# Adaptive-norm rows summed on VectorE instead of TensorE, and a projection moved into the recurrence, in a hybrid decoder layer

## What is computed

```python
mod = (c @ w_ada[l] + b_ada[l]).reshape(B, N_MOD, D)          # w_ada: 1024 x 6144
sh1, sc1, gt1, sh2, sc2, gt2 = [mod[:, i, None, :] for i in range(N_MOD)]
h = rms_norm(x, g_norm1[l]) * (1.0 + sc1) + sh1
proj = h @ w_in[l]
# branch A: short convolution, gated delta rule in chunks of 64 tokens -> o_a
# branch B: softmax attention with forget gates (fox)                   -> o_b
y = sigmoid(gate_a) * (o_a @ w_o_delta) + sigmoid(gate_b) * (o_b @ w_o_fox)
x = x + gt1 * (y @ w_out)
h = rms_norm(x, g_norm2[l]) * (1.0 + sc2) + sh2
x = x + gt2 * moe(h)          # 32 experts, top 4; then the final rms_norm
```

## Time and profile before

| | us |
|---|---|
| median of 3 runs | 1239.37 |
| lowest and highest | 1239.18, 1241.2 |
| the profiled execution, its own time | 1238.21 |
| span of its trace | 1236.4 |
| PE busy | 1138.6 (92%) |
| DVE busy | 316.1 (26%) |
| ACT busy | 184.7 (15%) |
| POOL busy | 106.0 (9%) |
| DMA, 462 MB in the main queue | 90.9% of 16 engines |

### The profile page before, as it was taken

One profiled execution on the slowest core, in us unless ns is written; L12 is line 12 of the kernel. 1 busy time (PEld: TensorE's weight loads), 2 busy tenths in 40 slices (PEclk: granted clock), 3 DMA queues, 4 the chain that ended last, 5 costly groups with the idle time before them and its releaser, 6 DMA issues.

```text
span 1236.4 us, 15283 instructions
## 1 busy us (share of the span) xinstructions
PE 1138.6 (92%) x6307; PEld 585.6 (47%) x6307; DVE 316.1 (26%) x674; ACT 184.7 (15%) x316; POOL 106.0 (9%) x50
## 2 busy tenths in 40 slices
PE   5999999999999999998989889898999999999896
PEld 2999799688543334333333323333434333333322
DVE  1633562131421221221212212121221222122102
ACT  2476344101310000010100000000000000000001
POOL 0764443110000000000000000000000000000000
PEclk9999999999999999999989999999999999999999
DMA  9963763597999999999999999999989999999995
GB/s 352 335 222 107 249 219 103 170 422 310 376 420 426 429 428 429 428 429 428 429 429 428 428 428 428 429 428 429 429 368 430 428 429 428 429 428 428 429 426 245
DMA packets 62558, 464.70 MB, mean 376 GB/s; under 512 B 8469, under 2 KB 31130, under 8 KB 34618
## 3 DMA queue, kind: packets, MB, share of 16 engines
q1 hardware_dynamic: 61256, 462.13, 90.9%
q10 hardware_dynamic: 1218, 1.93, 0.5%
q0 software_dynamic: 48, 0.13, 0.0%
HBM read 463.13 MB, written 1.05 MB: 375 GB/s over the span
## 4 chain that ended last, share of the span: by engine, by line
PE 64%; DMA 29%; issue 3%; ACT 2%; DVE 2%; SPq 0%; ACTq 0%; DVEq 0%
PE ps L488 61%; DMA ring<-in_w_down_dram 22%; DMA ring<-in_w_gate_up_dram 6%; PE ps L940 1%; ACT kept L1291 1%; DMA ring<-in_w_in_dram 1%; DMA ring<-in_g_onorm_dram 1%; PE ps L972 0%; PE ps L496 0%; ACT w_hi L1097 0%; DVE ring L1491 0%; SPq L358 0%; DVE ring L1485 0%; DVE ring L1775 0%; DVE kept L1717 0%
## 5 line engine op out<-in xcount | busy, mean ns | idle before, releaser
L488 PE MATMUL ps<-ring,kept 128*64 128x512 f32 (+1 forms) x3040 | 657.8, 600 | 36.1 <-DMA ring<-in_w_down_dram 22.5
L488 PEld LDWEIGHTS ps<-ring,kept 128*64 128x64 f32 (+1 forms) x3040 | 212.2, 138 | 454.3 <-issue 400.8
L488 PE MATMUL ps<-kept 128*128 128x128 f32 (+4 forms) x984 | 193.9, 413 | 8.5 <-ACT kept L1291 3.3
L488 PEld LDWEIGHTS ps<-kept 128*128 128x128 f32 (+2 forms) x984 | 108.5, 177 | 96.1 <-issue 81.0
L1287 ACT ACTIVATE kept<-kept 128x512 f32<-128x512 f32 x32 | 20.1, 629 | 731.4 <-DVE kept L1694 731.4
L1717 DVE TENSOR_TENSOR kept<-ps,kept 64x512 f32<-64x512 f32 x64 | 44.0, 688 | 298.4 <-PE ps L488 297.4
L1694 DVE TENSOR_SCALAR kept<-ps 128x512 f32<-128x512 f32 x32 | 22.1, 691 | 382.4 <-PE ps L488 382.4
L1787 POOL TENSOR_TENSOR w_lo<-ring,w_hi 128x1024 fp32r<-128x1024 f32 x38 | 91.8, 2434 | 108.2 <-ACT w_hi L1097 108.2
L488 PE MATMUL ps<-hT_hi,w_hi 128*128 128x256 f32 x272 | 78.7, 289 | 0.0
L488 PE MATMUL ps<-ring 64*64 64x64 f32 (+6 forms) x784 | 74.8, 270 | 3.0 <-issue 3.0
L488 PE MATMUL ps<-hT_lo,w_hi 128*128 128x256 f32 x272 | 77.0, 283 | 0.0
(11 more groups left out here) (227 smaller groups left out, 513.8 us busy)
## 6 DMA issues: line engine op xcount, KB each, us to landing
ring<-in_w_gate_up_dram SPq DMA_DIRECT2D x127, 2048.0 KB, 26.4
ring<-in_w_down_dram SPq DMA_DIRECT2D x47, 2048.0 KB, 23.8
kept<-in_w_down_dram SPq DMA_DIRECT2D x16, 2048.0 KB, 24.0
ring<-in_w_ada_dram SPq DMA_DIRECT2D x24, 1024.0 KB, 5.0
ring<-in_w_in_dram SPq DMA_DIRECT2D x22, 1024.0 KB, 11.5
ring<-in_w_out_dram SPq DMA_DIRECT2D x4, 1024.0 KB, 16.3
ring<-in_w_o_fox_dram SPq DMA_DIRECT2D x2, 1024.0 KB, 9.8
ring<-in_w_o_delta_dram SPq DMA_DIRECT2D x2, 1024.0 KB, 12.8
```

The source lines that it names most:

```text
L488: return pe.matmul(dst, lhsT, rhs, start=start, stop=stop, skip_group_check=True)
```

## The change

For ada part 1 and 2 DVE multiplies each unit (one row of `w_ada` in each partition) by its number of `c` and adds it to a running sum of 128x2048, `ada_sums` (`add_rows`: one TENSOR_SCALAR for the first unit of a part, seven SCALAR_TENSOR_TENSOR for the others, 16 instructions in all). PE then sums over the 128 partitions with a matrix of ones: four matmuls a part (`ada_over_rows`) instead of 32. The ada units now lie between the units of the projections in the ring; units that DVE uses are counted by a semaphore of their own, `ada_used`, and SP waits for the one or the other. The places of the recurrence where ada part 2 stood take two groups of the fox branch; the third comes behind the recurrence, and the transposes of the delta output stand in the middle of the fourth. Some semaphores are joined (`gate_ready` and `up_ready` into `gate_up_taken`, `counts_ps` into `route_ps`, `gfin_in` into `narrow_in`).

```diff
+        UNITS = [ada(0, k) for k in range(KD)]
+        UNITS += [dn(0), dn(1), dn(2), ada(1, 0), dn(3), dn(4), ada(1, 1), dn(5), fox(0), ada(1, 2), ada(1, 3)]
+        UNITS += [fox(1), fox(2), ada(1, 4), ada(1, 5), ada(1, 6), fox(3), ada(1, 7), ada(2, 0), fox(4), ada(2, 1)]
+        UNITS += [ada(2, 2), fox(5), ada(2, 3), ada(2, 4), zz(0), ada(2, 5), zz(1), ada(2, 6), ada(2, 7)]
         UNITS += [("gates", u, win_unit(COL_GATES + 256 * u)) for u in range(8)]
-        UNITS += [("ada2", k, ada_unit(2, k)) for k in range(KD)]
...
+        ada_sums = {1: arena(5120, UNIT), 2: arena(16292, UNIT)}
...
-                    sp.wait_ge(S("unit_used"), n - NSTREAM + 1)
+                    sp.wait_ge(S("ada_used" if SUMMED[n - NSTREAM] else "unit_used"),
+                               USED_AT[UNITS[n - NSTREAM][0:2]])
...
+            def ada_over_rows(part, b):
+
+                pe.wait_ge(S("ada_used"), KD * part)
+                for q in range(4):
+                    last = mm(ps[32 * q:32 * q + 32, b, :], km("ones")[:, 0:32],
+                              ada_sums[part][:, 512 * q:512 * q + 512], True, True)
+                last.then_inc(S("ada_summed"), 1)
...
             project("z", 0)
+            ada_over_rows(1, 5)
             project("z", 1)
+            mod_transposes(1, 6)
...
-            pe.wait_ge(S("rowF_taken"), 1)
-            ada(1, 5)
-            mod_transposes(1, 6)
+            pe.wait_ge(S("mod_cols_taken"), 2)
+            ada_over_rows(2, 6)
+            project("gates", 0)
...
             last.then_inc(S("U1_ps"), 1)
-            project("gates", 0)
-            pe.wait_ge(S("mod_cols_taken"), 2)
+            mod_transposes(2, 6)
+            pe.wait_ge(S("mod_cols_taken"), 3)
...
             between_state = {1: lambda: project("gates", LEVELS, (1,)), 2: lambda: project("gates", LEVELS + 1, (1,)),
-                             3: lambda: ada(2, 6, range(3, 6))}
+                             3: lambda: fox_branch(1)}
             between_vnew = {0: lambda: project("gates", LEVELS, (0,)), 1: lambda: project("gates", LEVELS + 1, (0,)),
-                            2: lambda: ada(2, 6, range(3)), 3: lambda: ada(2, 6, range(6, KD))}
+                            2: lambda: fox_branch(0), 3: lambda: None}
...
+            pe.wait_ge(S("yb_taken"), 1)
+            fox_branch(2)
...
+            pe.wait_ge(S("yb_taken"), 2)
+            branch_column(wf, obT, 1, 6)
+            pe.wait_ge(S("on_ready"), 1)
...
+            branch_column(wf, obT, 1, 7).then_inc(S("yb_ps"), 1)
...
+            def add_rows(part, k):
+
+                n = UNIT_AT[(f"ada{part}", k)]
+                dve.wait_ge(S(f"slot_in{n % NSTREAM}"), 16 * (n // NSTREAM + 1))
+                if k == 0:
+                    last = TS(ada_sums[part], unit_sb(n), vec("c", k), None, ALU.mult)
+                else:
+                    dve.wait_ge(S("ada_used"), KD * (part - 1) + k)
+                    last = STT(ada_sums[part], unit_sb(n), vec("c", k), ada_sums[part], ALU.mult, ALU.add)
+                last.then_inc(S("ada_used"), 1)
...
                 last.then_inc(S("conv_ready"), 1)
+                if u % 2 == 1:
+                    add_rows(1, u // 2)
+            add_rows(1, 3)
...
             ins.then_inc(S("cums_taken"), 1)
+            for k in range(4, 7):
+                add_rows(1, k)
...
             last.then_inc(S("rowF_taken"), 1)
+            add_rows(1, 7)
+            for k in range(5):
+                add_rows(2, k)
...
             last.then_inc(S("tok_taken"), 1)
+            for k in range(5, KD):
+                add_rows(2, k)
+            take_mod_rows(1, 5)
+            take_mod(1, 6)
...
             link(level(0))
+            dve.wait_ge(S("ada_summed"), 2)
```

More of the change, by code:

```diff
@@ L267, in rows_unit, with dn, fox, zz @@
             return (w[0, r0:r0 + kk * P, :].rearrange("(k p) n -> p k n", p=P), ("p (k n) -> p k n", dict(k=kk)))
-        UNITS = [("ada0", k, ada_unit(0, k)) for k in range(KD)]
-        UNITS += [("dn", u, win_unit(256 * u)) for u in range(6)]
-        UNITS += [("fqk", u, win_unit(COL_FOX + 256 * u)) for u in range(4)]
-        UNITS += [("fv", u, win_unit(COL_FOX + 2 * W + 256 * u)) for u in range(2)]
-        UNITS += [("z", u, win_unit(COL_Z + 256 * u)) for u in range(2)]
-        UNITS += [("ada1", k, ada_unit(1, k)) for k in range(KD)]
+        def dn(u):
+            return ("dn", u, win_unit(256 * u))
+        def fox(u):
+            return ("fqk", u, win_unit(COL_FOX + 256 * u)) if u < 4 else (
+                "fv", u - 4, win_unit(COL_FOX + 2 * W + 256 * (u - 4)))
+        def zz(u):
+            return ("z", u, win_unit(COL_Z + 256 * u))
+        def ada(part, k):
+            return (f"ada{part}", k, ada_unit(part, k))
+        UNITS = [ada(0, k) for k in range(KD)]
+        UNITS += [dn(0), dn(1), dn(2), ada(1, 0), dn(3), dn(4), ada(1, 1), dn(5), fox(0), ada(1, 2), ada(1, 3)]
+        UNITS += [fox(1), fox(2), ada(1, 4), ada(1, 5), ada(1, 6), fox(3), ada(1, 7), ada(2, 0), fox(4), ada(2, 1)]
+        UNITS += [ada(2, 2), fox(5), ada(2, 3), ada(2, 4), zz(0), ada(2, 5), zz(1), ada(2, 6), ada(2, 7)]
         UNITS += [("gates", u, win_unit(COL_GATES + 256 * u)) for u in range(8)]
-        UNITS += [("ada2", k, ada_unit(2, k)) for k in range(KD)]
         UNITS += [("wo_fox", u, rows_unit(w_o_fox, 256 * u, 2)) for u in range(2)]
@@ L281, in layer_kernel @@
         UNIT_AT = {(name, i): n for n, (name, i, _) in enumerate(UNITS)}
+        SUMMED = [name in ("ada1", "ada2") for name, _, _ in UNITS]
+        USED_AT = {(name, i): SUMMED[:n + 1].count(SUMMED[n]) for n, (name, i, _) in enumerate(UNITS)}
         WHOLE = 1
@@ L497, in _, with ada @@
                 last.then_inc(S("x_t"), 1)
-            def ada(part, b, ks=range(KD)):
+            def ada(b, ks=range(KD)):
                 for k in ks:
-                    w = unit_arrived(pe, f"ada{part}", k)
+                    w = unit_arrived(pe, "ada0", k)
                     for q in range(4):
@@ L523, in _ @@
             pe.wait_ge(S("cb_ready"), 1)
-            ada(0, 4, range(2))
+            ada(4, range(2))
             pe.wait_ge(S("xsq_ready"), 1)
@@ L529, in _ @@
             last.then_inc(S("xss_ps"), 1)
-            ada(0, 4, range(2, KD))
+            ada(4, range(2, KD))
             mod_transposes(0, 6)
@@ L765, in _, with branch_column, out_branch, fox_branch @@
             pe.wait_ge(S("hT_whole"), 1)
+            def branch_column(w, o, b, m):
+                for k in range(H):
+                    last = mm(bank(b, (m % 2) * T, T), w[k // 2][:, k % 2, m * P:(m + 1) * P], o[:, k, :],
+                              k == 0, k == H - 1)
+                return last
+            def out_branch(w, o, b, g, sem):
+                for m in (2 * g, 2 * g + 1):
+                    last = branch_column(w, o, b, m)
+                last.then_inc(S(sem), 1)
+            def fox_branch(g):
+                wf = [unit_arrived(pe, "wo_fox", u).rearrange("p (k n) -> p k n", k=2) for u in range(2)]
+                if g < 2:
+                    pe.wait_ge(S("proj_taken"), nproj[0] - 7 + g)
+                out_branch(wf, obT, g % 2, g, "yb_ps")
             between_state = {1: lambda: project("gates", LEVELS, (1,)), 2: lambda: project("gates", LEVELS + 1, (1,)),
-                             3: lambda: ada(2, 6, range(3, 6))}
+                             3: lambda: fox_branch(1)}
             between_vnew = {0: lambda: project("gates", LEVELS, (0,)), 1: lambda: project("gates", LEVELS + 1, (0,)),
-                            2: lambda: ada(2, 6, range(3)), 3: lambda: ada(2, 6, range(6, KD))}
+                            2: lambda: fox_branch(0), 3: lambda: None}
             for n in range(NCH):
@@ L1370, in take_mod_rows @@
             def take_mod_rows(part, b):
-                dve.wait_ge(S("unit_used"), UNIT_AT[(f"ada{part}", KD - 1)] + 1)
+                if part == 0:
+                    dve.wait_ge(S("unit_used"), USED_AT[("ada0", KD - 1)])
+                else:
+                    dve.wait_ge(S("ada_summed"), part)
                 CP(mod_rows, bank(b)).then_inc(S("mod_rows_sb"), 1)
```

66 lines of the change are left out of this document (24 added, 42 removed).

## The result

The changed kernel takes 1248.22 us (median of 7 runs, 1244.57 to 1251.02); the kernel before, run beside it, 1239.37 (median of 7, 1237.60 to 1242.17). The ratio is 1.0073, with a 95% interval from 1.0062 to 1.0085: slower by 8.9 us. 1248.5 was predicted. The profiled execution of the changed kernel has 1250.59 and a span of 1248.6, so it lies 2.4 above its median; before, the span was 1236.4. The trace thus has 12.2 us to explain, and the medians 8.9.

What follows compares the result with a forecast made beforehand. Expert weight bytes flowing from `out_ps` 4 bound the kernel; +22.6 before the level loop and -12.7 at the recurrence's end gave +9.9, 1248.1 from the profiled trace, stated as 1248.5 us, range 1232 to 1255 (forecast's own 1243 to 1253).

Steps and rivals of the forecast that it cites:

- the sum of +9.9: Whole kernel: 22.6 us lost before the level loop less 12.7 us won at the recurrence's end.
- What bounds the kernel: Expert stage: bound by weight bytes flowing from `out_ps` 4, so PE's time before 310 us counts one for one.
- Gain 1: End of the recurrence: fox groups replace ada part 2 pieces, so the delta branch starts 12.7 us earlier.
- The nine instructions on the path: Running-sums copy to keys: DVE takes turns with POOL, key transposes +16 us, value transposes +18 us.
- The TENSOR_SCALAR: First unit of an ada part on DVE: between 1.23 and 2.29 us, taken as 1.23.
- The four in the convolutions: Convolutions: four added DVE instructions fit in its waits for PE and were costed at nothing.
- Level 0 and `Xm`: Before the level loop: contention with the `gates` 0 and 1 subtractions adds 7.4 us; `Xm` ready at 170.8.
- The loop: Level loop: starts at 177.3 instead of 154.66, +22.6 us, and runs the same in both kernels.
- Gain 2: Around the level loop: ada part 1 shrinks on PE, net 4.6 us earlier if DVE had time.
- rival B: DVE beside POOL: no contention for these instructions, so -4.6 - 12.7 = -17.3, 1222 us; chance 0.08.
- Rival A: DVE beside POOL: DVE keeps its turn, loop at 162.5, total -4.9, 1234.5 us, faster; chance 0.20.
- Rival C: Ring slots: late DVE and landing waits delay ada units and `gates`, 5 to 8 us more, 1253 to 1256; chance 0.09.

Runs made afterwards that it cites:

- e1: The changed kernel with its fourteen SCALAR_TENSOR_TENSOR of add_rows replaced by one-input TENSOR_REDUCE, leaving out part of the conditioning sums; 2180.45 us, routing differs.
- e2: The kernel before plus nine extra two-input SCALAR_TENSOR_TENSOR of 128x2048 between the running-sums copy and the keys; 1258.15 us, ratio 1.0155.
- v3: The kernel before with late ada part 2 row sums, fox groups and semaphores moved/joined, fox group 0 taken earlier, two small instructions behind fox group four; 1228.67 us, 0.9913.
- v1: The kernel before with only ada part 2 as row sums, placed late, two fox groups in the recurrence and joined semaphores; 1232.38 us, ratio 0.9952.
- e3: The kernel before plus nine extra one-input TENSOR_REDUCE of 128x2048 between the running-sums copy and the keys; 1243.66 us, ratio 1.0040.
- e4: The kernel before plus only four extra two-input SCALAR_TENSOR_TENSOR of 128x2048 in the convolutions; 1240.75 us, ratio 1.0014.

## Why the prediction was right

The forecast was the likeliest case, and its mechanism held. That the time held to 0.3 us is in part luck: the sum of +9.9 stood for the profiled executions, and these lie 12.4 us apart (1238.21 and 1250.59), while the medians lie 8.9 apart. The last step of the working is also not clean: 1248.1 and the 1.2 by which the median lay above the execution make 1249.3, and 1248.5 was said.

- **What bounds the kernel.** Right. Over all kernels here but e1 the shift of SP's row gives the change of the time to within 2.5 us (e2 18.6 and 19.4, v3 -10.7 and -10.7, the change 10.9 and 8.9).
- **Gain 1**, 12.7: 13.2 by the traces, in the change and in e1 alike (the same group of the recurrence 4.0 us later, the loads 9.3 earlier). v1 keeps 8.7 us of it and v3 10.6, without the loss. The prediction called the mean clock of 0.79 "mostly the lower level", which it is not; but the three microseconds after it are at 0.50 in the trace, so its 1.7 us for the clock stand.
- **The nine instructions on the path**, +16 and +18: 137.5 and 141.5 were predicted for the key and value transposes, 137.27 and 141.53 measured. e1, e2 and e3 show that the turns make it. So close a match needs small errors that cancel: the stretch began 1.0 us later than assumed (95.71 for 94.7), the undisturbed duration, taken as 2.29 from a TENSOR_TENSOR of that size, is 2.34, and the waits inside the durations add up to about 16.4 us and not 18.1, since each of the eight subtractions costs DVE some 2.0 of its 2.4 us.
- **The TENSOR_SCALAR**, taken as 1.23: 1.28 alone, 3.43 in the stretch.
- **The four in the convolutions**, at nothing: e4 has 0.1%. In the changed kernel the copy of the running sums is 1.1 us later (95.59 for 94.51), in e4 0.4.
- **Level 0 and `Xm`**, `Xm` ready at 170.8: PE's transposes of X1 at 169.74. **The loop**, 177.3: 176.13. The forecast was 1.2 us too late there, since the turns of level 0 and `Xm` cost 5.6 us and not 7.4. But "In the loop both kernels do the same" left out the price of the clock: the loop's beginning takes 2.7 us more at the lower level. So the recurrence is 24.2 us late and not 22.6, and with gain 1 at 13.2 the loads are 10.9 late and not 9.9.
- **Gain 2**, "4.6 us earlier if DVE had time": this is the term that is not borne out. In e1, where the row sums lose no turns, the loop starts at 156.82, 2.2 later than before. The splits of `gates` 0 and 1 still collide with level 0 and `Xm`, which accounts for 5.2 of the 6.8 us that are missing (4.48 + 3.34 instead of 2.58). So rival B, whose 1222 was made of both gains in full, was mis-sized: e1's loads are 9.3 us earlier than before, which makes about 1230.
- **Rival A** (DVE keeps its turn) is out: wherever a subtraction waited, DVE's next `add_rows`, which stood ready, came behind it (the rows at 111.61, 122.02 and 126.40). The Trainium skill (SBUF — State Buffer, "Who interferes with whom") says that an instruction with two SBUF inputs contends with GpSimd's reads, that a TENSOR_REDUCE never does on this chip, and that who issues first has the whole instruction. The traces agree in each: 3077 ns against 2283 in the mean, and in e4 it is POOL that waits. What the sentence on the issue order leaves open, who is next when both queues are full, these rows answer: they alternate.
- **Rival C** (slots and landings): small. ACT waits 10.30 us for a landing of `w_in`, up to 109.83, but PE isn't late by it:

```profile
109.83 2.01 ACT L1127 ACTIVATE w_hi<-ring 128x1024 fp32r<-128x1024 f32 x2 [10.30 <-DMA ring<-in_w_in_dram]
```

## What to carry to other kernels

Before work is moved to VectorE because it idles there, read GpSimd's row over the same time: where GpSimd reads SBUF and the moved instruction has two SBUF inputs, GpSimd's instructions fall into VectorE's queue one by one (here 2.0 of the 2.4 us of each), and the free time is what both leave together. Place such work where GpSimd idles (v1), and keep even the tiniest two-input instruction off the path while GpSimd runs (v3: two of 0.15 to 0.17 us moved, the loads 3.8 us earlier). A gain at a late stage and a loss at an early one add up only in front of the point from which the stream flows; sum both there.
